# Adding expert outputs into the result expert by expert, on one Trainium2 core

## The reference, cut to what matters

```python
def grouped_experts(xn, eid, wt, w_gate, w_up, w_down):
    ...                                    # assignments sorted by expert, blocks of 128 rows
    def expert_block(args):
        xblk, e = args
        hid = jax.nn.silu(xblk @ w_gate[e]) * (xblk @ w_up[e])
        return hid @ w_down[e]
    yb = lax.map(expert_block, (xb, block_e)).reshape(n_slots, d)
    yb = (yb.astype(jnp.float32) * slot_w[:, None]).astype(xn.dtype)
    return jax.ops.segment_sum(yb, slot_tok, num_segments=n_tok)
...
    y = grouped_experts(xn, eid.reshape(-1), wt.reshape(-1), w_gate, w_up, w_down)
    return h + y.reshape(b, s, d)
```

## Time and profile before

| What | us |
|---|---|
| Median of 3 runs | 1868.04 |
| Lowest, highest run | 1862.54, 1869.71 |
| Profiled execution, own time | 1868.03 |
| Its span, first to last instruction | 1866.2 |
| TensorE busy | 1737.6 (93%) |
| VectorE busy | 1004.7 (54%) |
| ScalarE busy | 774.4 (41%) |
| GpSimd busy | 314.6 (17%) |

### The profile page before, as it was taken

How to read it: one execution, slowest core, us unless ns; L and a number is a source line. 1 busy time by engine, 2 the same in 40 slices (tenths; PEclk the granted TensorE clock), 3 DMA queues, 4 the chain that set the end, 5 groups by cost and what they waited for, 6 DMA issues and landing times.

```text
span 1866.2 us, 28130 instructions
## 1 busy us (share of the span) xinstructions
PE 1737.6 (93%) x11006; PEld 1560.5 (84%) x11014; DVE 1004.7 (54%) x1392; ACT 774.4 (41%) x1038; POOL 314.6 (17%) x344
## 2 busy tenths in 40 slices
PE   6999999999989999999999799649999999999980
PEld 5999988999979999888899788548888888888870
DVE  6104211277743233212365433359988989989874
ACT  5222211233332233222311222227888878878760
POOL 0001200000111113110101400012333333333310
PEclk9999999999989989999999999769999999999995
DMA  5322332222223223443654322339999999999957
GB/s 182 125 90 99 131 122 78 74 91 83 80 84 116 77 78 107 130 149 118 195 214 129 99 91 91 153 126 359 376 383 376 389 389 391 394 383 391 387 214 292
DMA packets 122881, 365.55 MB, mean 196 GB/s; under 512 B 19089, under 2 KB 79057, under 8 KB 96578
## 3 DMA queue, kind: packets, MB, share of 16 engines
q1 hardware_dynamic: 102210, 312.76, 46.1%
q0 software_dynamic: 19344, 46.99, 6.8%
q10 hardware_dynamic: 1232, 4.46, 0.6%
HBM read 330.41 MB, written 68.52 MB: 214 GB/s over the span
## 4 chain that ended last, share of the span: by engine, by line
PE 91%; DVE 3%; DMA 3%; ACT 1%; issue 1%; POOL 0%; SPq 0%; DVEq 0%; POOLq 0%; ACTq 0%
PE ps L789 15%; PE ps L790 15%; PE ps L791 15%; PE ps L1171 6%; PE ps L1173 6%; PE ps L1172 6%; PE ps L1194 3%; PE ps L1196 3%; PE ps L1195 3%; PE ps L1027 2%; PE ps L964 2%; PE ps L938 2%; PE ps L1160 2%; DMA out_y_prompt<-part 1%; PE ps L1029 1%; PE ps L948 1%
## 5 line engine op out<-in xcount | busy, mean ns | idle before, releaser
L789 PE MATMUL ps<-part,part 128*128 128x256 f32 (+3 forms) x1912 | 610.1, 319 | 11.8 <-DVE part L1781 7.4
L790 PE MATMUL ps<-part,part 128*128 128x256 f32 (+3 forms) x1912 | 595.9, 312 | 0.0
L791 PE MATMUL ps<-part,part 128*128 128x256 f32 (+3 forms) x1912 | 595.6, 312 | 0.0
L1897 DVE TENSOR_TENSOR part<-part,part 128x2048 fp32r<-128x2048 f32 x192 | 440.0, 2293 | 61.7 <-ACT part L1454 57.6
L1454 ACT ACTIVATE part<-part 128x2048 fp32r<-128x2048 f32 x192 | 368.2, 1919 | 116.4 <-PE ps L1173 82.5
L789 PEld LDWEIGHTS ps<-part,part 128*128 128x128 f32 x1912 | 368.7, 193 | 20.9 <-DVE part L1781 9.1
L790 PEld LDWEIGHTS ps<-part,part 128*128 128x128 f32 x1912 | 368.8, 193 | 4.8
L791 PEld LDWEIGHTS ps<-part,part 128*128 128x128 f32 x1912 | 367.9, 192 | 5.1
L1171 PE MATMUL ps<-part,part 128*128 128x512 f32 x512 | 203.6, 398 | 3.5 <-DVE part L1947 3.5
L1173 PE MATMUL ps<-part,part 128*128 128x512 f32 x512 | 200.5, 392 | 0.0
L1172 PE MATMUL ps<-part,part 128*128 128x512 f32 x512 | 200.2, 391 | 0.0
(11 more groups left out here) (229 smaller groups left out, 2018.0 us busy)
## 6 DMA issues: line engine op xcount, KB each, us to landing
part<-w_gate SPq DMA_DIRECT2D x64, 1024.0 KB, 8.0
part<-w_up SPq DMA_DIRECT2D x64, 1024.0 KB, 7.5
part<-w_down SPq DMA_DIRECT2D x64, 1024.0 KB, 7.3
part<-w_in SPq DMA_DIRECT2D x25, 1024.0 KB, 5.4
part<-x_prompt SPq DMA_DIRECT2D x16, 512.0 KB, 3.5
part<-expert_out_scratch SPq DMA_DIRECT2D x8, 1024.0 KB, 6.7
gate_scratch<-part POOLq DMA_DIRECT2D x32, 192.0 KB, 3.0
part<-gate_scratch SPq DMA_DIRECT2D x4, 1088.0 KB, 6.4
```

The source lines that it names most:

```text
L789: mm(out, lhs[0](k), rhs[0](k), start=(k == 0), stop=False)
L790: mm(out, lhs[0](k), rhs[1](k), start=False, stop=False)
L791: last = mm(out, lhs[1](k), rhs[0](k), start=False, stop=(k == n - 1))
L1897: tt(elo[:, off % NSPL, :], eraw[:, off % NRAW, :], ehi[:, off % NSPL, :].bitcast(F32), ALU.subtract)\
```

## The change

The expert rows no longer go to a scratch tensor. POOL stores the residual tiles `hbuf` into the two outputs early, beside the stores of `x2`. For each expert in turn POOL gathers the present output rows of its tokens into `acc` (one indirect DMA for the sample output, then one for the prompt output), adds `yb` (POOL, 128x1024), and scatters `acc` back (two indirect DMAs). The weight of each row is applied by ACT as it evacuates PSUM, from a new table `wtab` that 18 more matmuls build (float32). For the last expert DVE does the addition straight out of PSUM. The next expert's output rows are read only when both stores of the one before have landed (`y_st`). `y_evac(b)` now waits for the addition of expert b-1 (`acc_done`) instead of its store. The gather of expert b+2 stands at the head of POOL's turn b, behind the stores of turn b-1. The index copies are gone, the loops over experts on SP, ACT, DVE and POOL are written out, the final pass is gone, and `eraw` has 12 slots, of which five load at once, three once `hbuf` is stored, and four once the second table and the first gather are there.

```diff
-    NRAW, NSPL = 6, 3
+    NRAW, NSPL, EARLY = 12, 3, 8
...
         def load_chunks(plan, b):
             for kind, j, off, expert in plan:
-                if not isinstance(b, int) or 6 * b + off >= NRAW:
-                    sp.wait_ge(s("e_split"), b * 6 + (off - NRAW + 1))
-                load_chunk(kind, j, expert, off % NRAW)
+                c = 6 * b + off
+                if c == 5:
+                    sp.wait_ge(s("h_st"), 16 * TILES)
+                if c == EARLY:
+                    sp.wait_ge(s("table_ready"), 2)
+                    sp.wait_ge(s("xg_in"), 16)
+                if c >= NRAW:
+                    sp.wait_ge(s("e_split"), c - NRAW + 1)
+                load_chunk(kind, j, expert, c % NRAW)
...
+        pe.wait_ge(s("onehot"), 2)
+        for i in range(2 * TILES):
+            last = mm(ps[:, 3, 2 * SLOTB:3 * SLOTB], in_row[:, i, :].bitcast(F32), w_col[:, i, :], start=(i == 0), stop=(i == 2 * TILES - 1))
         last.then_inc(s("tab_mm"), 1)
...
-        def y_evac(b, used, first=False):
+        def y_evac(b, used):
             act.wait_ge(s("e_used"), used)
-            if not first:
-                act.wait_ge(s("y_st"), b * 16)
-            act_(yb, flat(5)[:, 0:D], ACT.Copy).then_inc(s("y_read"), 1)
+            if b > 0:
+                act.wait_ge(s("acc_done"), b)
+            act_(yb, flat(5)[:, 0:D], ACT.Copy, scale=wtab[:, b:b + 1]).then_inc(s("y_read"), 1)
...
+        step(tt(wts_v, wts[:, :, :], cst[:, CVALID:CVALID + TILES].unsqueeze(2).to_broadcast([P, TILES, 2]), ALU.mult))
+        tt(w_col, in_col, wts_v.rearrange("p t j -> p (t j)").unsqueeze(2).to_broadcast([P, 2 * TILES, SLOTB]), ALU.mult)\
+            .then_inc(s("onehot"), 1)
...
+        dve.wait_ge(s("tab_mm"), 2)
+        cp(wtab[:, :], ps[:, 3, 2 * SLOTB:3 * SLOTB]).then_inc(s("table_ready"), 1)
...
+        dve.wait_ge(s("e_used"), 6 * NE)
+        dve.wait_ge(s("acc_in"), 32 * NE)
+        stt(acc, flat(5)[:, 0:D], wtab[:, NE - 1:NE], acc, ALU.mult, ALU.add).then_inc(s("y_read"), 1)
...
             dma(xn_d[col0(t):col0(t) + w, :], x2[i % 2][0:w, :]).then_inc(s(f"x2_st{i % 2}"), 16)
+            y_rows = o["y_sample"].rearrange("b s d -> (b s) d") if t == ST else o["y_prompt"][0, P * t:P * t + P, :]
+            dma(y_rows, hbuf[0:w, t, :]).then_inc(s("h_st"), 16)
...
+        def add(k):
+            nc.gpsimd.tensor_tensor(acc, acc, yb, ALU.add).then_inc(s("acc_done"), 1)
+            pool.wait_ge(s("acc_done"), k)
+
+        def store_acc(idx_p, idx_s):
+            pool.indirect_dma_start(y_p, at(idx_p), acc, None, bounds_check=NPROMPT - 1, oob_is_err=False).then_inc(s("y_st"), 16)
+            pool.indirect_dma_start(y_s, at(idx_s), acc, None, bounds_check=NSAMP - 1, oob_is_err=False).then_inc(s("y_st"), 16)
+
+        gather(tabt[:, 0:1])
+        pool.wait_ge(s("xg_tr"), 1)
+        gather(tabt[:, 1:2])
+        pool.wait_ge(s("table_ready"), 2)
+        pool.wait_ge(s("h_st"), 16 * TILES)
+        for b in range(NE):
+            if b + 2 < NE:
+                pool.wait_ge(s("xg_tr"), b + 2)
+                gather(tabt[:, b + 2:b + 3])
+            idx_p, idx_s = tabp[:, b:b + 1], tabt[:, b:b + 1]
+            if b > 0:
+                pool.wait_ge(s("y_st"), 32 * b)
+            load_acc_s(idx_s)
+            pool.wait_ge(s("acc_in"), 32 * b + 16)
+            load_acc_p(idx_p)
+            if b < NE - 1:
+                pool.wait_ge(s("acc_in"), 32 * (b + 1))
+            pool.wait_ge(s("y_read"), b + 1)
+            if b < NE - 1:
+                add(b + 1)
+            store_acc(idx_p, idx_s)
+        pool.wait_ge(s("y_st"), 32 * NE)
```

More of the change, by code:

```diff
@@ L334, in _build @@
     num_col = lr.take(2 * TILES, SLOTB, dt=F32R)
+    wts_v = lr.take(TILES, 2)
+    w_col = in_col
     assert lr.at <= AFTER_M
-    NRAW, NSPL = 6, 3
+    NRAW, NSPL, EARLY = 12, 3, 8
     CW = 2048
     le_ = Lay(0)
-    eraw = le_.take(NRAW, CW)
     ehi = le_.take(NSPL, CW, dt=F32R)
     elo = le_.take(NSPL, CW, dt=F32R)
+    eraw = [le_.take(CW) for _ in range(5)]
+    assert le_.at <= 2 * KT * T + WSLOT + 4 * D
     xg = le_.take(D)
@@ L349, in _build @@
     hTl = le_.take(4, P, dt=F32R)
[L350 to L355, removed]
+    assert le_.at <= AFTER_W
+    eraw += [Lay(AFTER_M + 2 * D + CW * i).take(CW) for i in range(EARLY - 5)]
+    eraw += [Lay(AFTER_W + CW * i).take(CW) for i in range(NRAW - EARLY)]
+    lf = Lay(AFTER_H)
+    yb, acc = lf.take(D), lf.take(D)
+    tabp, wtab, wcur = lf.take(SLOTB, dt=I32), lf.take(SLOTB), lf.take(1)
+    E_IN = [f"e_in{i}" for i in range(NRAW)]
     ps = ctx.enter_context(nc.psum_tensor("ps", [P, 8, 512], F32))
@@ L725, in _, with load_chunk @@
         sp.wait_ge(s("out_mm"), TILES)
-        def load_chunk(kind, j, expert, slot6):
+        def load_chunk(kind, j, expert, slot):
             if kind == "gu":
@@ L755, in _ @@
                     eo = sp.value_load(obe[0:1, bass.ds(j2, 1)], min_val=0, max_val=NE - 1)
[L756 to L763, removed]
+                    for kind, j, off, expert in over_chunks(eo):
+                        sp.wait_ge(s("e_split"), (j2 + (NE - 1)) * 6 + (off + 1))
+                        load_chunk(kind, j, expert, off)
         sp.wait_ge(s("cache_out"), 16 * len(pieces))
@@ L1147, in _ @@
         mm(ps[:, 2, 0:NE], nbb[0:NE, 0:P], cbf[0:NE, BLS:BLS + NE], start=True, stop=True)
[L1148 removed]
+        mm(ps[:, 2, NE:2 * NE], nbb[0:NE, 0:P], cbf[0:NE, BLI:BLI + NE], start=True, stop=True).then_inc(s("count_mm"), 1)
         pe.wait_ge(s("onehot"), 1)
@@ L1485, in _, with turn @@
         hid_hi(0)
-        def turn(b, bn, last=False):
+        def turn(b):
             for off in (1, 2, 3, 4):
@@ L1491, in turn @@
             silu(b, b * 6 + 2)
-            if not last:
+            if b + 1 < NE:
                 xg_hi(b + 1)
             c_hi(b, 5)
-            if not last:
+            if b + 1 < NE:
                 c_hi(b, 6)
-            y_evac(b - 1, b * 6 + 4, first=(bn == 1))
+            if b == 1:
+                act.wait_ge(s("table_ready"), 2)
+            y_evac(b - 1, b * 6 + 4)
             hid_hi(b)
[L1500 to L1504, removed]
+        for b in range(1, NE):
+            turn(b)
         act.wait_ge(s("table_ready"), 1)
@@ L1512, in _ @@
                     for off in range(6):
-                        c_hi(b, off)
+                        c_hi_over(j2, off)
                     silu(b, b * 6 + 4)
                     hid_hi(b)
[L1516 to L1524, removed]
+                    act.wait_ge(s("e_used"), b * 6 + 6)
+                    act.wait_ge(s("idx_ready"), j2 * 3 + 3)
+                    act.wait_ge(s("acc_done"), j2 + (NE - 1))
+                    act_(yb, flat(5)[:, 0:D], ACT.Copy, scale=wcur[:, 0:1]).then_inc(s("y_read"), 1)
     @block.vector
@@ L1979, in turn @@
             hid_lo(b)
-        with dve.Fori(1, NE - 1) as b:
-            turn(b)
-        turn(NE - 1, last=True)
+        for b in range(1, NE):
+            turn(b, last=(b == NE - 1))
+        dve.wait_ge(s("e_used"), 6 * NE)
+        dve.wait_ge(s("acc_in"), 32 * NE)
+        stt(acc, flat(5)[:, 0:D], wtab[:, NE - 1:NE], acc, ALU.mult, ALU.add).then_inc(s("y_read"), 1)
         nover = dve.value_load(obe[0:1, OVER:OVER + 1], min_val=0, max_val=OVER)
@@ L1990, in _ @@
                     for off in range(6):
[L1991 removed]
+                        c_lo_over(b, off)
                     hidden(b)
                     hid_lo(b)
[L1995 to L2002 removed]
     @block.gpsimd
@@ L2124, in _, with gather @@
-        with pool.Fori(3, NE) as b:
-            pool.wait_ge(s("xg_tr"), b)
-            gather(b, b * 2 - 3)
-            store(b - 3, b * 2 - 2)
-        for i in range(3):
-            store(NE - 3 + i, 2 * NE - 3 + i)
+        y_p, y_s = o["y_prompt"][0], o["y_sample"].rearrange("b s d -> (b s) d")
+        at = lambda idx: bass.IndirectOffsetOnAxis(ap=idx, axis=0)
+        def gather(idx):
+            pool.indirect_dma_start(xg, None, xn_d, at(idx), bounds_check=T - 1, oob_is_err=False).then_inc(s("xg_in"), 16)
```

89 lines of the change are left out of this document (46 added, 43 removed).

## The result

| | before | changed |
|---|---|---|
| median us | 1866.94 (4 runs) | 2218.21 (4 runs, 2209.4 to 2221.96) |
| span of the profiled execution | 1866.2 | 2220.1 |

The ratio is 1.188 (95% interval 1.184 to 1.192): slower by 351 us, where 246 were forecast. It is inside the range of 1930 to 2256, above the likeliest case's 2068 to 2198. One execution of one experiment (b_fin9) took 4342 us where its eleven others took 1852 to 1864, and it is left out of that comparison.

A forecast was written before the change was run, and what follows sets the result against it. TensorE was taken to bound the expert loop at 17.75 us a turn, DMAs the final pass. A period of 27.1 us adds 271 us over 29 turns and the end saves 25: 1868.0 + 271 - 25 = 2114 us, range 1930 to 2256.

The forecast's parts named there:

- the likeliest case: Expert loop: the wait through the late gather sets a period of 25.5 to 30 us, 2068 to 2198 us; chance 0.42.
- the ring: Expert loop, x_tr to next x_tr: evacuation, addition, two stores, gather in series; 24.0 us, 27.1 with the slowed clock.
- the second rival: Expert loop: POOL's own waits or its queue set the period, 30 to 33 us, 2198 to 2285 us; chance 0.18.
- One sign that I had written down against myself: POOL in the expert loop: the forecast would be wrong if POOL waited mostly for y_st and the output rows.
- Two further signs: Expert loop: gathers issued about 18 us after x_tr, right behind two stores; DMA rate near 250 GB/s.
- Two stores' issues: POOL, ahead of the gather: each issue keeps POOL for 1.02 us, 2.0 together, at most 6.
- The gather: Expert loop, issue to landing behind two stores: 9 us taken, bounds 4.2 and 15.8, some relief when TensorE stops.
- The addition: POOL, 128x1024: 2.7 us taken from 2.25, 2.7 and 8.1; 4.5 if it waits for a DVE split.
- The clock: TensorE behind each stop: 6 us at half clock, costing 3.1 us a turn.
- The second ring: POOL alone: stores landed, sample rows, prompt rows, addition; 24.3 us expected, 15.8 at the least, 33.3 all contended.
- The end: From x_tr(31) to the end of the span: 57 us taken against 81.8, so 25 us less.
- the second table: Before the expert loop: extra matmuls lie mostly beside the first gather; between -3 and +1 us, 0 taken.

The follow-up runs named there:

- b_fin9: Kernel before, with nine input and nine output buffers in the final pass instead of three and two: 1859.8 us, ratio 0.996.
- a_order: Changed kernel, with the gather issued ahead of the wait for the evacuation: 2074.7 us, ratio 1.109.
- b_late: Kernel before, with only store(b-3) put ahead of gather(b) in POOL's loop: 2124.7 us, ratio 1.137.
- a_nolo: Changed kernel, with DVE's split cut from 2048 to 64 columns from the fourth chunk on: 2116.9 us, ratio 1.132.
- a_perm4: Changed kernel, experts reordered, output rows loaded turns ahead, wait for stores of b-1 and sample-row load moved behind the stores of b: 1879.5 us, ratio 1.006.
- a_warm: Changed kernel, with 46 filler matmuls ahead of each x_tr in the loop to keep TensorE busy: 2172.5 us, ratio 1.163.
- a_noload: Changed kernel, gather ahead of the evacuation wait and output rows' loads left out, so nothing is accumulated: 1849.2 us, ratio 0.990.
- a_perm3: Changed kernel, experts reordered, three acc buffers, gather first, output rows loaded ahead of the addition of b: 1885.3 us, ratio 1.010.
- a_thin: Changed kernel, with every weight load behind the first twelve cut to 256 bytes a partition: 2080.1 us, ratio 1.113.

## Why the prediction was right, and where it was off

The mechanism and its place were right: TensorE waits at every `x_tr` for the gather behind two stores, 29 times, at half clock after each stop. a_order and b_late show it from both sides. The forecast was 104 us low, by the sizes of the ring's terms. By these the mean turn, 30.68 us, left the 25.5 to 30 of my likeliest case and fell where I had put the second rival (over 30, chance 0.18). One sign that I had written down against myself came as well: POOL waited longer for its stores and the output rows (158.1 + 136.9 us) than for ACT (237.1). It was a poor sign: POOL waits for ACT in all 30 turns, 7.9 us each, so its own ring has slack, and the gather is what TensorE waits for. Two further signs came near: the gather is issued 20.4 us behind `x_tr` at the median, not 18, and the DMA engines move 231 GB/s in the 29 turns, not 250. The sum, term by term:

| Term of the ring | predicted us | turn from 1362.84 |
|---|---|---|
| `x_tr` to the end of the evacuation, with the clock | 9.2 + 3.1 | 11.67 |
| to POOL | 0.2 | 0.14 |
| addition | 2.7 | 3.45 |
| to the first store | 0.9 | 0.82 |
| two stores issued | 2.0 | 4.69 |
| gather, issue to landing | 9 | 10.31 |
| sum | 27.1 | 31.08 |

- *Two stores' issues* is the term that was mis-sized most: 2.7 of the 4.0 us that were missing, 78 us of 29 turns. The 1.02 of the earlier trace rows is the median of stores that came, in the old order, 0.9 us behind an index copy that had itself waited for a split (1.29 us in the earlier trace rows, where the shortest of the 32 copies takes 0.18). In the new order each of the two meets a split of its own, and the gap between two indirect DMAs is 0.30 us, which I had put at nothing. a_nolo gives 1.03 and 0.99 without splits.
- *The gather*: I took 9 for some relief when TensorE stops. There was none, 10.3 us: the loads issued late in a turn drain just while TensorE waits (387 GB/s in the last window). The extra delay that I had as an upper end, for two stores ahead in the same queue, is small: 0.3 us against the earlier trace rows, or 1.1 if the shorter issue is set against it (1.9 us here, 2.7 there).
- *The addition*: 3.45, not 2.7. The Trainium skill, "SBUF — State Buffer", on the shared port pair, says that a GpSimd operation that reads SBUF (the on-chip memory) and a DVE operation with two SBUF inputs exclude each other for the whole instruction. The trace agrees in kind: 2.41 us with the splits cut, 3.44 with them, and in a_perm4 the split is the one that waits. The 4.5 us was an upper end (it is one split on top of the least, 2.25; on top of my 2.7 it would be 5.0): in nearly every turn some 1.0 us of a split is left when the addition comes.
- *The clock* cost up to 2.5 us in the turn shown, and 1.6 a turn by a_warm, not 3.1: it stayed at 0.50 for 4 to 5 us, not 6.
- *The second ring*: forecast 24.3 us, measured 25.8 when the first was open, and then it was the bound.
- *The end*: 57 forecast, 59.5 measured, of which the last 5.3 lie behind the landing of the last store and were not in the forecast; *the second table*: 0 forecast, 1.3 measured, its 18 float32 matmuls took 7.93 us, beside the first gather as written; *slots*: nothing, as written.

What stays open: what fills the 10.6 us behind a_noload's last store (the profile shows nothing there), whether POOL's ring or DVE's longer splits set a_perm3's turn, and how much the accumulation costs at best. a_perm4's waits between its two loads could be taken away only by loading both halves of a buffer at once, which was not tried on the chip, since the two would write one buffer unordered.

## What to carry to other kernels

An operation that hands out the next turn's input belongs ahead of everything in its queue that waits for this turn's output; write the ring of waits from one such hand-out to the next, with measured durations, before adding to it. Replacing one pass at the end by a read-modify-write in each turn turns bytes that flowed at 294 GB/s here (364 with more buffers) into latencies of 4 to 10 us in series, and latencies are paid every turn. Take an issue's duration from the place in the order where it will stand: the same instruction took 1.0 or 2.2 us, by what DVE did at that moment.

## What the runs showed of the hardware that was not expected

- POOL's issue of an indirect DMA takes 1.0 us alone and 1.9 to 2.2 us beside DVE's two-input splits, and not only the addition is held up.
- An indirect load of the few sample rows of an expert (4 on average: 64 tokens, two experts each, 32 experts) lands no sooner than one of its prompt rows (64 on average): 4.8 us at the median for line 2124 against 4.2 for line 2127. The two stand at different places of a turn, but with the weight loads thin (a_thin) it is 4.5 against 4.2.
- Behind a turn's stop of some 10 us TensorE's granted clock is 0.50 for 4 to 5 us. Filler matmuls in the stop keep it at 1.00, and are worth 1.6 us a turn where the next work is on the critical ring.
- A gather with two stores ahead of it on POOL's queue landed 10.3 us after its issue against 10.0 without them.
